# Hymba/PEER step on one core: tile 0 first through out-projection and head 0, row buffers and copies reordered

## The reference

```
hp = rms_norm(xp, norm_mix) * (1 + sc1) + sh1
qa, ka, va, qb, kb, vb = project_qkv(hp, w_in)            # w_in: 1024 x 3072
oa, ob = stick_breaking(qa, ka, va), dilated_attention(qb, kb, vb)
xp = xp + g1 * (concat(rms_norm(oa), rms_norm(ob)) @ w_out)
hp2 = rms_norm(xp, norm_ffn) * (1 + sc2) + sh2
# PEER, 8 heads: 2 x 128 sub-key scores, top 16 of each, top 16 of the 256 sums
q = (hp2 @ w_peer_q).reshape(t, 8, 2, 128)
s = einsum('thcd,hcnd->thcn', q, sub_keys)
expert = i1 * 128 + i2                                    # 16 of 16384 experts per token and head
act = gelu(einsum('thkd,td->thk', peer_u[expert], hp2))
xp = xp + g2 * einsum('thk,thkd->td', softmax(c_top) * act, peer_v[expert])
y = rms_norm(xp, norm_final)
```

## Time and profile before

| | before |
|---|---|
| median of 3 runs | 1185.79 us (1184.83 to 1186.88) |
| the profiled execution, its own time | 1189.29 us |
| its span in the trace | 1187.5 us |
| busy: PE / DVE / ACT / POOL | 904.6 / 608.9 / 328.9 / 417.6 us |
| moved by the DMA engines | 481.28 MB, mean 405 GB/s |

### The profile page before, as it was taken

The page is one execution under the profiler, slowest core; times in us unless marked ns, Lnnn a source line. Parts: engine busy times, 40 slices in busy tenths (PEclk is TensorE's granted clock), DMA queues, the critical chain, the costliest instruction groups (busy, mean ns, idle before and its releaser), DMA issues. The chain is left out here.

```text
span 1187.5 us, 13078 instructions
## 1 busy us (share of the span) xinstructions
PE 904.6 (76%) x3693; PEld 422.0 (36%) x3693; DVE 608.9 (51%) x1602; ACT 328.9 (28%) x939; POOL 417.6 (35%) x432
## 2 busy tenths in 40 slices
PE   2798598678758877877778697777877777777685
PEld 0343243444323445433334253233323232332232
DVE  2200100443223537555555555777777777777766
ACT  1000001642122012333232323333333333333333
POOL 1201133213121002334342343455555555545542
PEclk9899799868788889899898899999999999999987
DMA  9999999999999997999999999999999999999997
GB/s 362 441 387 405 329 405 412 413 392 379 398 404 385 395 323 260 426 427 428 428 429 429 428 428 427 428 427 426 427 426 428 427 427 426 427 427 428 428 400 320
DMA packets 71600, 481.28 MB, mean 405 GB/s; under 512 B 9753, under 2 KB 10106, under 8 KB 25858
## 3 DMA queue, kind: packets, MB, share of 16 engines
q0 software_dynamic: 55008, 378.58, 77.1%
q1 hardware_dynamic: 16514, 102.10, 21.7%
q10 hardware_dynamic: 32, 0.02, 0.0%
HBM read 477.41 MB, written 70.32 MB: 461 GB/s over the span
## 5 line engine op out<-in xcount | busy, mean ns | idle before, releaser
L975 PE MATMUL ps<-R,diag 128*128 128x512 f32 x1024 | 497.4, 636 | 156.4 <-ACT diag L1287 156.3
L484 POOL DMA_INDIRECT R<-in_uv,idst x256 | 306.5, 1197 | 370.7 <-PE ps L975 321.8
L1801 DVE CUSTOM_DVE_ANT_0 R<-R,H 128x1024 f32<-128x1024 f32 x264 | 320.6, 1224 | 205.7 <-DMA R<-in_uv,idst 197.5
L975 PEld LDWEIGHTS ps<-R,diag 128*128 128x128 f32 x1024 | 199.4, 202 | 440.7 <-ACT diag L1287 226.6
L1261 ACT ACTIVATE gel<-dots 128x2 f32<-128x2 f32 (+1 forms) x133 | 27.0, 203 | 407.4 <-DVE dots L1801 407.4
L592 PE MATMUL ps<-R,HT 128*128 128x512 f32 x192 | 93.7, 627 | 5.7 <-DMA R<-in_wts 5.7
L1287 ACT ACTIVATE diag<-const,wgt 128x128 f32<-128x128 f32 x256 | 88.8, 394 | 8.6
L308 POOL DMA_DIRECT2D R<-in_sb_k x64 | 34.7, 542 | 88.0 <-issue 87.4
L317 POOL DMA_INDIRECT R<-in_sb_v,vrow x32 | 30.4, 950 | 97.8 <-PE ps L751 84.8
L1264 ACT ACTIVATE wgt<-gel,gst 128x1 f32<-128x1 f32 x264 | 63.4, 287 | 4.5 <-ACT gel L1261 0.2
L928 PE MATMUL ps<-HT,R 128*128 128x264 f32 x256 | 61.4, 396 | 0.7 <-ACT HT L1025 0.7
(11 more groups left out here) (290 smaller groups left out, 815.4 us busy)
## 6 DMA issues: line engine op xcount, KB each, us to landing
R<-in_wts POOLq DMA_DIRECT2D x48, 1024.0 KB, 15.0
out_dil_k_s<-in_dil_k SPq DMA_DIRECT2D x32, 1023.5 KB, 7.6
out_dil_v_s<-in_dil_v SPq DMA_DIRECT2D x32, 1023.5 KB, 7.9
R<-in_sb_k SPq DMA_DIRECT2D x64, 256.0 KB, 8.7
R<-in_sb_k POOLq DMA_DIRECT2D x64, 256.0 KB, 6.5
R<-in_win_v SPq DMA_DIRECT2D x8, 512.0 KB
R<-in_uv,idst POOLq DMA_INDIRECT x256, 12.3
R<-in_win_k SPq DMA_DIRECT2D x1, 1926.0 KB, 14.5
```

The costliest lines, as they stand in the source:

```text
L484: pool.indirect_dma_start(out=R[:, row_slot(k), :], out_offset=None, in_=A["uv"], in_offset=bass.IndirectOffsetOnAxis(ap=idst[:, par, k:k ...
L975: last = pe.matmul(ps[:, banks + q, :], diag[:, k % 4, :], R[:, row_slot(k), D + q * 512:D + (q + 1) * 512], start=False, stop=False, skip ...
L1801: dve.tensor_tensor_reduce(u, u, H[:, t, :], 1.0, 0.0, ALU.mult, ALU.add, dots[:, k:k + 1]).then_inc(s["dot_done"], 1)
```

## The change

- **Copies.** `EARLY, GAP, PACED` go from 16, 20, 42 to 11, 15, 27: 11 pieces instead of 16 in the key stage, 4 as before at the start of the value stage, 12 instead of 22 from its end on, and 37 instead of 22 in PEER.
- **Tile 0 first.** PE turns tile 0 alone before `out_bank(0)`, tile 1 before `out_bank(1)`. After `out_bank(2)` it turns tile 0's normed input, makes head 0's queries and scores for tile 0 alone (128 columns, into `q0_mm`, `sc0_mm`), and only then the samples' rows, `out_bank(3)` and tile 1. DVE chooses head 0's experts of tile 0 right after `residual(2)`; the rest of tile 1's norm is the new function `second_tile`, after that choice. The two groups' sums of the merge norm are split by group.
- **Keys of head 0.** A new buffer `subk0` holds the sub-keys of head 0 (128 KB), loaded by SP ahead of the constants; the other keys still wait for `h_ready` 6.
- **Rows.** The slot order becomes 4, 5, 7, 0, 1, 2, 3, 6. The first three rows need no wait, the next four only the end of `out_bank(3)`; row 7 uses slot 6, which holds head 0's query weights. Query weights lie in slots 6, 8, 9, 8, ... instead of 5, 6, 7, 8, 9, 8, ...
- **Heads.** Two heads instead of three are queried ahead of the experts; heads 2 and 3 go beside head 0's experts (`two_heads`).

```diff
-EARLY, GAP, PACED, PACE = 16, 20, 42, 4
+EARLY, GAP, PACED, PACE = 11, 15, 27, 4
+ROWS = (4, 5, 7, 0, 1, 2, 3, 6)
...
-            return k % NSLOT
+            return ROWS[k % NSLOT]
...
+            sp.dma_start(subk0[:, :, :], A["subk"][:, 0:2 * NKEY].rearrange("p (g n) -> p g n", g=2)).then_inc(s["small_in"], 16)
...
+            head_ids(0, 0)
+            for k in range(NSLOT - 1):
+                if row_slot(k) < WSLOTS:
+                    pool.wait_ge(s["w_used"], QUERIES - WSLOTS + row_slot(k) + 1)
+                head_row(0, k)
+            pool.wait_ge(s["h_ready"], 6)
+            pool.dma_start(subk, A["subk"].rearrange("p (g n) -> p g n", g=16)).then_inc(s["subk_in"], 16)
+            pool.wait_ge(s["w_used"], QUERIES + 1)
+            head_row(0, NSLOT - 1)
+            pool.wait_ge(s["w_used"], QUERIES + 2)
+            query_weight(3, 8)
+            for k in range(NSLOT, TOPK):
+                pool.wait_ge(s["e_used"], k - NSLOT + 1)
+                head_row(0, k)
...
-            for n in range(4):
+            for n in range(2):
                 merge_ev(n)
...
+            def two_heads(h):
+
+                return {1: lambda: query_group(h, 0), 3: lambda: query_group(h, 1),
+                        5: lambda: score_group(h, 0), 7: lambda: score_group(h, 1),
+                        9: lambda: query_group(h + 1, 0), 11: lambda: query_group(h + 1, 1),
+                        13: lambda: score_group(h + 1, 0), 15: lambda: score_group(h + 1, 1)}
...
-            for i in range(2):
-                all_of(choose(i, scores=2 * i + 2))
-            with dve.Fori(0, NH - 2) as h:
+            all_of(choose(0, scores=1, ready="sc0_ev"))
+            second_tile()
+            dot_rows(0, 0, rows=NSLOT)
+            all_of(choose(1, scores=4))
+            dot_rows(0, 0, first=NSLOT, beside=choose(2, scores=6), at=(9, 11, 13, 15))
+            with dve.Fori(1, NH - 2) as h:
                 dot_rows(h, 0, beside=choose(h + 2, scores=2 * h + 6))
```

More of the change, by code:

```diff
@@ L936, in score_group @@
                     pe.wait_ge(s["score_ev"], m - 1)
-                for t in range(2):
+                for t in range(2) if h else (1,):
                     last = pe.matmul(ps[:, 2 + j, t * P:(t + 1) * P], eq[:, j, t * P:(t + 1) * P],
-                                     subk[:, m, :], start=True, stop=True)
+                                     subk[:, m, :] if h else subk0[:, j, :], start=True, stop=True)
                 last.then_inc(s["score_mm"], 1)
@@ L1189, in _ @@
                 half_turned(0, half, half, s["hT_ev"])
[L1190 to L1193, removed]
-                last = act.activation(hT[:, bass.ds(b, QUADS, step=2), SEQ:NTOK],
-                                      ps[:, 7, b * P:(b + 1) * P].rearrange("p (k n) -> p k n", k=QUADS)[:, :, 0:NB], ACT.Copy)
-            last.then_inc(s["hT_ev"], 1)
-            for half in range(2):
-                act.wait_ge(s["hT_mm"], half + 4)
-                half_turned(1, half, (2, 5)[half], s["hT_ev"])
             def query_ev(h, j):
@@ L1212, in query_ev @@
                                ps[:, j, SEQ:NTOK].rearrange("p (a n) -> p a n", a=1).to_broadcast([P, 2, NB]), ACT.Copy)
-                act.activation(eq[:, j, 0:SEQ], ps[:, j, 0:SEQ], ACT.Copy).then_inc(s["pq_ev"], 1)
+                left = slice(0 if h else P, SEQ)
+                act.activation(eq[:, j, left], ps[:, j, left], ACT.Copy).then_inc(s["pq_ev"], 1)
             def score_ev(h, j):
@@ L1238, in _ @@
             act.wait_ge(s["z_v"], 1)
-            for h in range(3):
+            for j in range(2):
+                act.wait_ge(s["q0_mm"], j + 1)
+                act.activation(eq[:, j, 0:P], ps[:, j, 0:P], ACT.Copy).then_inc(s["q0_ev"], 1)
+            act.wait_ge(s["sc0_mm"], 1)
+            act.activation(S[:, 0, :, :], ps[:, 5, 0:2 * NKEY].rearrange("p (c n) -> p c n", c=2), ACT.Copy).then_inc(s["sc0_ev"], 1)
+            top_exp(0)
+            root(3, 2)
+            root(4, 1)
+            act.wait_ge(s["hT_mm"], 3)
+            for b in range(2):
+                last = act.activation(hT[:, bass.ds(b, QUADS, step=2), SEQ:NTOK],
+                                      ps[:, 7, b * P:(b + 1) * P].rearrange("p (k n) -> p k n", k=QUADS)[:, :, 0:NB], ACT.Copy)
+            last.then_inc(s["hT_ev"], 1)
+            for half in range(2):
+                act.wait_ge(s["hT_mm"], half + 4)
+                half_turned(1, half, 2 + half, s["hT_ev"])
+            for h in range(2):
                 for j in range(2):
@@ L1297, in _ @@
                 head_weights(h, first=(h == 0), top=h + 2,
[L1298 removed]
+                             beside=two_heads(2) if h == 0 else next_head(h + 3) if h < 5 else {3: decode_score_ev, 7: decode_rows_ev} if h == 5 else None)
             with act.Fori(0, NH - 1) as h:
@@ L1793, in choose, with dot_rows @@
                 assert tk.n == TOPSTEPS, tk.n
-            def dot_rows(i, t, rows=TOPK, beside=(), at=range(3, TOPK, 4)):
+            def dot_rows(i, t, rows=TOPK, beside=(), at=range(3, TOPK, 4), first=0):
                 parts = iter(beside)
-                for k in range(rows):
+                for k in range(first, rows):
                     dve.wait_ge(e_ready[k % NSLOT], i * 32 + 16 * (k // NSLOT + 1))
```

214 lines of the change are left out of this document (120 added, 94 removed).

## The result

The changed kernel takes 1194.08 us in the median of 12 runs (1190.31 to 1199.22), the kernel before beside it 1185.67 (12 runs, 1181.08 to 1190.84): a ratio of 1.0069, 95% interval 1.005 to 1.0088. It is slower by 0.7%; the forecast was 1190.7 us, 0.4% slower. The profiled execution has a span of 1194.9 us, against 1187.5.

The account below looks back on a forecast made before the run. Transfers at 427 GB/s were taken to bound PEER; 1187.5 - 17 - 26.5 + 45.4 + 3 = 1192.4 us of span, then + 1.8 - 3.5 = 1190.7 us, 0.4% slower, range 1183 to 1198.

Parts of the forecast that it names:

- What bounds the kernel: In PEER, transfers set the pace at 427 GB/s; each 1 MB copy, head row or weight chunk costs 2.45 us.
- The rival that copies beside rows are free: In PEER, copies beside head rows cost nothing, so 36.8 us comes off, giving 1154 us; chance 0.03.
- Step 1: Key stage: five copies fewer let the key page leave earlier, net -17 us, bounds -12 and -19.
- the rival of the value stage: Value stage: half of PE's 23.4 us wait for value rows goes, 11.7 us, giving 1179 us; chance 0.12.
- Step 2: Out-projection to PEER: the first head row goes out 26.5 us earlier, bounds 24 and 28.
- Step 3: From the first head row on: 18.5 pieces more to move at 2.45 us each, +45.4 us.
- Step 4: Start of PEER: a second gap in the transfers after the first seven rows, +3 us, bounds 0 and 8.
- no choice waits: Start of PEER: DVE's choice of head 1, 11.55 us, is covered by 24 us of rows and copies under way.
- PEER starves at its start: Start of PEER: row 7, sub-keys and head 1's scores chain behind seven rows, 8 to 10 us more, 1200; chance 0.09.

Follow-up runs that it names:

- a fast kernel with 33: The changed kernel with 33 copies instead of 27, the sub-keys on SP's queue, and head 1's exponentials after expert 3 instead of 7: 1180.37 us, 0.9936.
- the last kernel: The changed kernel with 37 copies, sub-keys on SP's queue ahead of the last four, and head 1's exponentials after expert 3 instead of 7: 1184.16 us, 0.9977.

## Why the prediction was right, step by step

**What bounds the kernel.** Confirmed: 426 GB/s from 480 to 740, with copies, and 427 from 900 to 1120, without (the last copy leaves at 899.36, 481 us after the first row, where some 475 was forecast). The rival that copies beside rows are free is out: ten copies fewer moved ahead of PEER in the old order lengthen the rest by 762.6 - 738.0 = 24.6 us, 2.46 each, where 2.45 was used.

**Step 1, five copies fewer (-17).** The stall of 18.46 us became three waits of 0.71, 0.53 and 1.99 and four matmuls at half the clock (3.47 instead of 1.98). The first copy after the value stage leaves at 357.36, 14.7 earlier than before; the last merge of heads, on DVE, starts 16.9 earlier. In the kernel before, and in the changed one:

```profile
383.37 0.86 DVE L1557 TENSOR_SCALAR QKV<-ps,stat 128x64 f32<-128x64 f32 x4 [0.84 <-PE ps L801]
```

```profile
366.51 0.86 DVE L1610 TENSOR_SCALAR QKV<-ps,stat 128x64 f32<-128x64 f32 x4 [0.84 <-PE ps L814]
```

The size fits by the second mark, in part by luck. The key stage itself, up to its last page scores on PE, ends only 13.1 us earlier:

```profile
223.19 1.07 PE L619 MATMUL ps<-R,Z 128*32 128x256 f32 x16
```

```profile
210.10 1.07 PE L632 MATMUL ps<-R,Z 128*32 128x256 f32 x16
```

The rest came in the value stage. Two waits of PE in the changed kernel stand against each other (total, times, longest):

```profile
PE ps L764 <- DMA R<-in_sb_v,vrow: 17.3, 7, 7.6
PE ps L581 <- DMA const<-in_consts: 13.5, 1, 13.5
```

The wait for the constants was 10.6 us before: with `subk0` ahead of them it grew by 2.9, where 0.8 was put. The other profiles bear this out: 10.4 to 11.0 in the three of the old order, 12.9 to 13.5 in the nine of the new. The price of the five copies shows without it in the new order: with 16 of them the key stage ends at 226.13, with 11 at 207.7 to 210.7, so 17 us, where 17.5 was put. The wait for value rows was 23.4 and is 6.1 shorter, half of what the rival of the value stage asked for. But in the nine other kernels with 11 copies in the key stage it is 16.9 to 25.0, 21.3 on the mean, so most of these 6 us belong to the one profile, and what the rival asked for isn't there.

**Step 2, the first head row (-26.5).** From the merge to the first row: 462.73 - 383.37 = 79.4 us before, 418.71 - 366.51 = 52.2 after, so -27.2. It repeats: 50.8 to 52.3 us in the nine profiles of the new order, 75.8 to 79.4 in the three of the old. `out_bank(0)` took 10.02, the choice 417.67 - 406.13 = 11.5. The queries took 3.84 us (3.2 put, bounds up to 3.7), and their price was misread: the trace shows each of these matmuls twice. The 16 of tile 0 (L927) are x32 there, and so the 7.29 us of 32 rows are one head of 16 matmuls and not two. Read rightly the upper bound was 7.3 us; that 3.2 came near is luck. Steps 1 and 2 together: 44.0 us where 43.5 was forecast.

**Step 3, what is left to move (+45.4).** The hole came where it was put: last copy at 397.44, 96 GB/s from 396 to 418. The old order with the constants of the change prices it without the rest of the change: 1.5% slower. Filling the hole with 33 copies, 5.5 more by the first row, gives back 13.9 us by the rests (776.2 - 762.3), 5.5 x 2.45 = 13.5 by this step. The bytes themselves agree: the engines moved 382 GB/s up to the first row before and 377 in the changed kernel, of 481.3 and 481.4 MB in all, so 304 MB were left before and 324 now, 19 to 20 MB more, or 45 to 47 us at 427 GB/s.

**Step 4, the start of PEER (+3).** The term that was mis-sized: the rest is 776.2 - 724.8 = 51.4 us longer, less 45.4 that is 6.0 us, inside the bounds of 0 and 8. The gap is the one described: from 418 to 460 the engines fell short by (427 - 344) / 427 x 22 + (427 - 327) / 427 x 20 = 9.0 us, against 3 before. PE's first expert was put at 464 in the old clock, 447 in the actual one, and came at 448.61. The transfers were put to last as long, and didn't fill the 20 us up to 460. PE's part was too small by the same misreading: its queries for two heads were put at 7.3 us, and took 5.55 for head 0 (136 columns, from 428.12) and then, for head 1,

```profile
434.44 7.29 PE L958 MATMUL ps<-HT,R 128*128 128x264 f32 x32
```

12.8 us in all, up to 441.7. So the sub-keys on POOL's queue held PE up by only 2.5 us here, and taking this wait away moved the first reuse of a slot by 2.6. The rest of the 6.0 us wasn't taken apart. That no choice waits was wrong: DVE waited 9.84 us for ACT's exponentials, though moving them gained nothing in the changed kernel.

**The sum.** -14.7 and -29.3 to the first row, or -16.9 and -27.2 by the other mark, then 45.4 and 6.0: +7.4 us of span, where +4.9 was forecast. The sum came out well although `subk0`, the queries and the start of PEER cost more than was put; the value stage, shorter by chance in this profile, made up for a part of it. The rival "PEER starves at its start" was half true: it doesn't decide here, and takes up to 10 us as soon as copies run beside the first rows. That is the part which neither the forecast nor the first expectations had. It is also why the new order with 37 copies (0.9998) was no better than the old one with as many (0.997, intervals that overlap): its first row is 30.8 us earlier, 20.8 of them go into 8.5 pieces more that are left to move, and 8.5 more are lost at the start. With the sub-keys moved it is at 0.9928.

## What to carry to other kernels

Where transfers set the pace, a change pays by the moment at which the pace begins less the bytes that it leaves for it: count, stage by stage, what the queues hold while the compute chain runs, and refill a stage that is shortened to its new length (here 6 of 10 copies; the other four did no harm only with the sub-keys ahead of them). At the seam ask which single transfer the first buffer release hangs on, and give it the queue that is short. An operation moved ahead in an in-order engine's list must be moved no further than its operand can be ready in the slowest case: after expert 3 it changed nothing with 27 copies, stood in a fast kernel with 33 (ACT waited 3.82 us there; not tried apart), and cost 6 to 7 us with 37 (1184.16 against 1177.07).

## What the runs showed of the hardware

The same megabyte, asked for at nearly the same time (426.39 and 423.36), landed after 30.1 us behind seven head rows on POOL's queue, beside copies on SP's, and after 8.9 us on SP's, where the copy ahead of it had just landed and two more left behind it. The traffic was shared between the two queues, not served in the order of issue: the sub-keys landed at 432.3, and a head row that POOL had asked for at 420.56, 2.8 us before them, at 443.3, when DVE began on it:

```profile
443.34 1.22 DVE L1861 CUSTOM_DVE_ANT_0 R<-R,H 128x1024 f32<-128x1024 f32 x1 [6.77 <-DMA R<-in_uv,idst]
```

The Trainium skill says so (DMA: Bandwidth & Descriptors, "Queues, rings and completion order"): each DMA engine takes turns between the queues that have work. These numbers agree with it, though nothing here shows the size of a turn. The limit of about 358 GB/s a core that the same page gives for HBM to SBUF ("Where 436 GB/s comes from") doesn't hold here: the changed kernel moves 426 GB/s from 480 to 740 us, with copies, and 427 from 900 to 1120, where only head rows are fetched.

A change of ACT's function has its price as well: two loads of a table, 1.28 us each, stand around head 1's exponentials in the last kernel (at 455.26 and 473.19).
